# A list of 16 blocks for the recurrent part of a hybrid decoder block: projections two blocks ahead, dealt out between the levels, four value tiles a block, 64 keys at level 32

## The chip, the core and the metric

One core of a Trainium2 chip runs the whole program in one launch. The metric is the time on the device in microseconds (us), lower is better. Names used below: PE is TensorE (matmuls; PEld its weight loads), DVE is VectorE, ACT is ScalarE, POOL is GpSimd, SP is SyncE, which here only starts DMA transfers. Each engine works through its own queue in the order of the program and waits on semaphores for the others.

## The reference

The block takes x (2048 x 1024), norms it, projects it to 4096 columns, and runs two mixers beside each other: a gated linear recurrence (4 heads of 128) and a mixture of dilated window attentions (8 heads of 64). Both are gated, joined, projected and normed. All in float32. The part that the change touches is the recurrence:

```python
def hgrn2_mixer(q, f_logit, i, lb):
    log_f = jnp.logaddexp(jnp.log(lb), jnp.log1p(-lb) + jax.nn.log_sigmoid(f_logit))
    k = -jnp.expm1(log_f)
    q = jax.nn.silu(q)
    ...
    def step(state, inp):
        qc, kc, vc, gc = inp
        b = jnp.cumsum(gc, axis=2)
        o_inter = jnp.einsum('bhck,bhkv->bhcv', qc * jnp.exp(b), state)
        diff = b[:, :, :, None, :] - b[:, :, None, :, :]
        decay = jnp.exp(jnp.where(causal, diff, -jnp.inf))
        scores = jnp.einsum('bhtk,bhtsk,bhsk->bhts', qc, decay, kc)
        o_intra = jnp.einsum('bhts,bhsv->bhtv', scores, vc)
        ...
        new_state = jnp.exp(b_last[:, :, 0, :])[..., None] * state + \
            jnp.einsum('bhsk,bhsv->bhkv', k_dec, vc)
        return new_state, o_inter + o_intra
```

Behind it the readout is normed per head, multiplied by a gain and by silu of a gate z.

## The kernel before

The program has a prologue (the norm of x, its transposes, and the values and gates of head 0), the recurrent part, a short dense part (values of the attention), the attention and the output projection. Every float32 projection is done as three matmuls per 128 rows of depth on operands split in a high and a low half: hi by hi, hi by lo, lo by hi (lines 632 to 634), 24 matmuls in a group.

The recurrent part has four units, one per head. A unit has four blocks of 512 time steps, each of four chunks of 128. The order of the work is a list, `HG_STEPS`, that every engine walks; each engine does its share of a step:

- P: the queries of a block into bank 0 and its forget gates into bank 1, 24 matmuls of 512 columns each (PE). ACT takes the sigmoid of the queries (line 1024), DVE multiplies them (`q_read`).
- K: ACT takes two sigmoids of the forget gates (1032, 1033), POOL scales them (1249, 1250).
- L: DVE builds the decays and the scaled queries and keys for the five levels (half widths 4, 8, 16, 32, 64), lines 1440 to 1503, and signals `lev_ready` at its end.
- M: PE turns the keys (693) into bank 4, multiplies keys by queries for the five levels (704; 701 three times; 707), alternating between banks 2 and 3, and multiplies keys by values (716). DVE takes each level out of its bank (1516, 1521, 1524/1525, 1527) and says so with `lev_read`, which PE waits for two levels later; then it carries the states on (1535). ACT copies the turned keys out (1037).
- O: PE reads out (724, 726) to bank 6; ACT squares (1043); POOL takes the root (1258, 1260). Z: DVE norms and gates (1545) and SP stores.
- T: one value tile of the next unit: 24 matmuls of 256 columns (PE), into bank 7 for even tiles and bank 4 for odd ones; ACT copies it out and takes the sigmoid (987, 988, `sig_done`); in units 0 to 2 POOL gates it (1199, 1201, `gated`), in unit 3 (the tiles are the attention's first values) it does not; SP stores it. A tile may start when the tile two before it is out.

M needs bank 4 for the turned keys, so it waits for the last odd tile in front of it: `pe.wait_ge(sig_done, u * 16 + (16 + odd_before("M", b)))`. The numbers of tiles in front of the four M steps of a unit are 5, 7, 9 and 15, so the last tile before an M is always an even one, in bank 7.

The weights come in pieces: SP loads one of two staging buffers (362, `load_piece`), ACT makes the high half (972, `split_hi`), POOL the low half (1186, `split_lo`). The pieces of the values (slot 0) go in at P of block 0. Those of the next unit's queries and forget gates (slot 1) go in at the value tiles 8, 10, 11 and 13, behind the last P of the unit: SP starts a piece's load ahead of that tile's store, ACT splits it behind that tile's copy. A unit ends with DVE's, ACT's and POOL's steps for block 3; the next one begins with P for block 0 and P for block 1 one behind the other.

Of the kernel before, what the change touches and what calls it, by code (L numbers as in the profile page):

```python
# [11 lines left out]
ALU = mybir.AluOpType  # L12
ACT = mybir.ActivationFunctionType

P = 128
# [8 lines left out]
GC = 256  # L24
# [18 lines left out]
HG_STEPS = ([("P", 0), ("K", 0), ("L", 0), ("P", 1)] + [("T", t) for t in range(5)]  # L43
            + [("M", 0), ("K", 1), ("L", 1), ("P", 2), ("O", 0), ("T", 5), ("T", 6)]
            + [("M", 1), ("Z", 0), ("K", 2), ("L", 2), ("P", 3), ("O", 1), ("T", 7), ("T", 8)]
            + [("M", 2), ("Z", 1), ("K", 3), ("L", 3), ("T", 9), ("O", 2)] + [("T", t) for t in range(10, 15)]
            + [("M", 3), ("Z", 2), ("T", 15), ("O", 3), ("Z", 3)])
SPLIT_AT = {"prologue": (1, 4, 7, 10), "hgrn": (8, 10, 11, 13)}


def tiles_before(kind, b):

    return sum(k == "T" for k, _ in HG_STEPS[:HG_STEPS.index((kind, b))])


def odd_before(kind, b):

    return tiles_before(kind, b) // 2 * 2


def blocks_before(kind, tile):

    return sum(k == kind for k, _ in HG_STEPS[:HG_STEPS.index(("T", tile))])

# [41 lines left out]
def build(nc, x, w_groups, w_units, w_out, norm_w, gate_g, lb_logits, final_w, rope, near_mask, far_mask, tri_masks, out):  # L106
# [7 lines left out]
    with ExitStack() as ctx:  # L114
# [155 lines left out]
        passed_sp, passed_dve, passed_pool = sem("passed_sp"), sem("passed_dve"), sem("passed_pool")  # L270
        rs_half, dve_step, pool_step = sem("rs_half"), sem("dve_step"), sem("pool_step")
# [78 lines left out]
        def _(sp):  # L350
# [45 lines left out]
            for step in range(TILES + 5):  # L396
                if step >= 5:
                    phase1_store(0, step - 5)
                if step - 3 in SPLIT_AT["prologue"]:
                    load_piece(1, SPLIT_AT["prologue"].index(step - 3))  # L400
# [4 lines left out]
            def hg_unit(u, last):  # L405
                def load_vg(b):
                    if b == 0:
                        after(vg_stored[0], u * 128 + 128)
                        after(vg_stored[1], u * 128 + 128)
                    after(out_stored[b % 2], u * 32 + (16 * (b // 2) + ONE))  # L410
                    src = vg_dram[bass.ds(u, 1), b * BT:(b + 1) * BT, :]
                    sp.dma_start(vg_blk[b % 2], src.rearrange("a (c t) n -> (a t) c n", c=CH))\
                        .then_inc(vg_loaded[b % 2], 16)

                for kind, i in HG_STEPS:
                    if kind == "P":
                        if i == 0:
                            load_piece(2 * u + 2, 0)
                            load_piece(2 * u + 2, 1)
                            load_vg(0)  # L420
                            load_piece(2 * u + 2, 2)
                            load_piece(2 * u + 2, 3)
                            load_vg(1)
                    elif kind == "Z":
                        after((out_done0, out_done1)[i % 2], u * 2 + (i // 2 + 1 + ONE))
                        dst = mixed_dram[i * BT:(i + 1) * BT, bass.ds(u * P, P)]
                        sp.dma_start(dst.rearrange("(c t) n -> t c n", c=CH), vg_blk[i % 2][:, :, P:GC])\
                            .then_inc(out_stored[i % 2], 16)
                        if i < 2:
                            load_vg(i + 2)  # L430
                    elif kind == "T":
# [1367 lines left out]
```

## Time and profile before

| what | us |
|---|---|
| median of 3 runs | 1357.95 (1350.57 to 1358.93) |
| the profiled execution's own time | 1354.28 |
| its span, first to last instruction | 1352.3 |
| recurrent part on PE, first P to the end of the last O | 496.2 (81.97 to 578.18) |
| granted clock of PE, mean | 0.996 of 2.4 GHz |

The profile is one execution. The busy time of PE counts a matmul from its start to its modelled end, and the ends overlap with the next starts; so the distance between starts is what a matmul costs, and the text works with these. "idle before" stands in brackets behind a row with the one that ended it. Between the span and the execution's own time lie 2.0 us that the change doesn't touch.

### The profile page before, as it was taken

The page shows a single profiled execution, that of the slowest core. Times are in us where ns is not written, and L with a number is a line of the kernel's source. Part 1 is how long each engine was busy: PE and PEld are TensorE (multiplying, and loading weights), DVE is VectorE, ACT ScalarE, POOL GpSimd, SP SyncE. Part 2 cuts the span into 40 slices and gives each one's busy share as a digit, 9 for nine tenths or more (in the row PEclk, how much of TensorE's full clock was granted, in tenths as well). Part 3 has the DMA queues.
Part 4 walks back from the last instruction along what each step waited for, and adds up shares of the span by engine and source line. Part 5 has one row for each costly group of instructions (what it writes and reads, how often), then busy time and mean ns, then how long its engine had stood idle before and what let it go on. Part 6 is the DMA issues. An engine that isn't in the chain of part 4 may idle for free.

```text
span 1352.3 us, 23456 instructions
## 1 busy us (share of the span) xinstructions
PE 1300.5 (96%) x8520; PEld 1138.6 (84%) x8520; DVE 711.5 (53%) x1885; ACT 464.2 (34%) x1328; POOL 436.3 (32%) x441
## 2 busy tenths in 40 slices
PE   5999999999999999999999999999999999999997
PEld 5989998988889799999878877887788877878886
DVE  5837783776578378720445545544455456333332
ACT  5721122212212211221445445544545457411111
POOL 5742343333424312230134433443343344102000
PEclk9999999999999999999999999999999999999999
DMA  6520123013202301234355545554545566535431
GB/s 207 164 82 20 40 79 86 24 48 93 71 17 78 106 20 32 87 113 112 75 141 134 126 104 142 134 126 108 141 131 124 140 175 182 176 119 182 135 117 63
DMA packets 121714, 143.89 MB, mean 106 GB/s; under 512 B 20352, under 2 KB 86400, under 8 KB 121600
## 3 DMA queue, kind: packets, MB, share of 16 engines
q1 hardware_dynamic: 119200, 138.46, 36.5%
q10 hardware_dynamic: 2400, 3.93, 1.1%
q8 instruction: 69, 1.13, 0.4%
q14 instruction: 45, 0.37, 0.1%
HBM read 87.56 MB, written 29.62 MB: 87 GB/s over the span
## 4 chain that ended last, share of the span: by engine, by line
PE 76%; DMA 9%; DVE 8%; issue 2%; POOL 2%; ACT 2%; SPq 1%; ACTq 0%; DVEq 0%; POOLq 0%
PE bank L632 9%; PE bank L634 8%; PE bank L633 8%; PE bank L764 5%; PE bank L766 5%; PE bank L765 5%; PE bank L792 4%; PE bank L794 4%; PE bank L793 4%; DMA qd<-turned 4%; PE bank L871 3%; DMA stage<-in_w_groups 3%; PE bank L924 3%; PE bank L862 2%; PE bank L701 2%
## 5 line engine op out<-in xcount | busy, mean ns | idle before, releaser
L632 PE MATMUL bank<-w_hi,u_hi 128*128 128x256 f32 x768 | 221.2, 288 | 2.0 <-POOL w_lo L1186 1.5
L633 PE MATMUL bank<-w_lo,u_hi 128*128 128x256 f32 x768 | 218.1, 284 | 0.0
L634 PE MATMUL bank<-w_hi,u_lo 128*128 128x256 f32 x768 | 218.1, 284 | 0.0
L1368 DVE TENSOR_TENSOR room<-room 128x256 f32<-128x256 f32 (+6 forms) x386 | 135.2, 397 | 40.3 <-POOL room L1250 36.8
L632 PEld LDWEIGHTS bank<-w_hi,u_hi 128*128 128x128 f32 x768 | 148.1, 193 | 4.2 <-DVE u_lo L1368 1.7
L633 PEld LDWEIGHTS bank<-w_lo,u_hi 128*128 128x128 f32 x768 | 148.2, 193 | 0.2
L634 PEld LDWEIGHTS bank<-w_hi,u_lo 128*128 128x128 f32 x768 | 148.0, 193 | 0.0
L764 PE MATMUL bank<-u_hi,w_hi 128*128 128x512 f32 x256 | 108.7, 425 | 0.0
L1368 DVE TENSOR_TENSOR t<-bank,tab 128x512 f32<-128x512 f32 x64 | 42.6, 687 | 123.8 <-DMA tab<-in_rope 52.6
L632 PE MATMUL bank<-u_hi,w_hi 128*128 128x512 f32 x256 | 101.5, 397 | 5.2 <-ACT room L1033 2.4
L1282 POOL TENSOR_TENSOR r<-t,t 64x512 f32<-64x512 f32 x16 | 35.0, 2189 | 219.5 <-DVE w L1636 208.5
L766 PE MATMUL bank<-u_hi,w_lo 128*128 128x512 f32 x256 | 102.1, 399 | 0.0
L792 PE MATMUL bank<-u_hi,mT_hi 128*128 128x512 f32 x256 | 101.9, 398 | 0.0
L765 PE MATMUL bank<-u_lo,w_hi 128*128 128x512 f32 x256 | 101.7, 397 | 0.0
L794 PE MATMUL bank<-u_hi,mT_lo 128*128 128x512 f32 x256 | 100.0, 391 | 0.0
L634 PE MATMUL bank<-u_hi,w_lo 128*128 128x512 f32 x256 | 99.9, 390 | 0.0
L793 PE MATMUL bank<-u_lo,mT_hi 128*128 128x512 f32 x256 | 99.7, 390 | 0.0
L633 PE MATMUL bank<-u_lo,w_hi 128*128 128x512 f32 x256 | 99.6, 389 | 0.0
L1088 ACT COPY pT<-bank 128x512 f32<-128x512 f32 x60 | 35.3, 588 | 176.7 <-PE bank L885 176.7
L1605 DVE CUSTOM_DVE_ANT_0 p_near<-bank,near_m 128x256 f32<-128x256 f32 (+1 forms) x128 | 48.1, 411 | 85.3 <-PE bank L885 57.2
L871 PE MATMUL bank<-ks,qd 128*128 128x128 f32 (+3 forms) x256 | 88.6, 350 | 0.0
L1186 POOL TENSOR_TENSOR w_lo<-stage,w_hi 128x512 fp32r<-128x512 f32 x44 | 58.3, 1331 | 84.6 <-ACT w_hi L972 84.6
(169 smaller groups left out, 2936.0 us busy)
## 6 DMA issues: line engine op xcount, KB each, us to landing
qd<-turned SPq DMA_DIRECT2D x64, 256.0 KB, 4.7
stage<-in_w_groups SPq DMA_DIRECT2D x44, 256.0 KB, 3.9
room<-in_x SPq DMA_DIRECT2D x16, 512.0 KB, 4.4
values_gates<-vg_tile SPq DMA_DIRECT2D x64, 128.0 KB, 1.7
room<-values_gates SPq DMA_DIRECT2D x16, 512.0 KB, 4.7
tab<-in_rope SPq DMA_DIRECT2D x16, 512.0 KB, 5.7
wide<-mix_weights SPq DMA_DIRECT2D x32, 256.0 KB, 3.9
xr<-in_x SPq DMA_DIRECT2D x16, 512.0 KB, 4.9
```

What stands on the lines that cost most here:

```text
L632: nc.tensor.matmul(dst, lhs_hi(k), rhs_hi(k), start=(k == 0), stop=False)
L633: nc.tensor.matmul(dst, lhs_hi(k), rhs_lo(k), start=False, stop=False)
L634: last = nc.tensor.matmul(dst, lhs_lo(k), rhs_hi(k), start=False, stop=(k == KT_N - 1))
L764: yield nc.tensor.matmul(bk[:, :], wh[:, k, :], u_hi[:, k, sl], start=(k == 0), stop=False)
L765: yield nc.tensor.matmul(bk[:, :], wh[:, k, :], u_lo[:, k, sl], start=False, stop=False)
L766: last = nc.tensor.matmul(bk[:, :], wl[:, k, :], u_hi[:, k, sl], start=False, stop=(k == KT_N - 1))
L792: yield nc.tensor.matmul(bk[:, :], mT_hi[t % 2][:, k, :], wo_hi[half][:, k, :], start=(k == 0), stop=False)
L793: yield nc.tensor.matmul(bk[:, :], mT_hi[t % 2][:, k, :], wo_lo[half][:, k, :], start=False, stop=False)
L794: last = nc.tensor.matmul(bk[:, :], mT_lo[t % 2][:, k, :], wo_hi[half][:, k, :], start=False, stop=(k == KT_N - 1))
L871: last = nc.tensor.matmul(bank[2 + h][:, 0:P * (g + 1)], q[h][:, z, j::CH], keys, start=(z == 0), stop=(z == 1))
L1186: nc.gpsimd.tensor_tensor(w_lo[slot][:, 2 * i:2 * i + 2, :], stage[i % 2][:, :, :], w_hi[slot][:, 2 * i:2 * i + 2, :].bitcast(F32), ALU.su ...
L1368: return nc.vector.tensor_tensor(dst, a_, b_, op)
```

## The change

The list becomes one of 16 blocks over all units, without a loop over units. For block n (unit u, block b) it has: M; K and L of n+1; P of n+2; O; the value tiles; Z. At the seams of the units the next unit's P's now stand in the last two blocks of this one. The value tiles of a unit are dealt 4, 4, 4, 4 to its blocks (unit 0: 4 in front, then 3 a block; unit 3: 2, 2, 6, 6). The numbers of tiles in front of the M steps are now 4, 7, 10, 13, then 16, 20, 24 and so on by 4 up to 48, then 50, 52, 58. The two splits have steps of their own: G and V (load and split of the value weights), H and W (load and split of the query and forget weights).

```diff
+def hg_steps():
+    steps = [("N", 0, 0), ("G", 0, 0), ("G", 0, 1), ("P", 0, 0)] + [("V", 0, i) for i in range(2)]
+    steps += [("G", 0, 2), ("G", 0, 3), ("K", 0, 0), ("L", 0, 0), ("P", 0, 1)]
+    steps += [("V", 0, 2), ("V", 0, 3)] + [("T", 0, t) for t in range(4)]
...
+        if b == 1:
+            steps += [("H", u, 0), ("H", u, 1)]
+        steps.append(("O", u, b))
+        if b == 1:
+            steps += [("W", u, 0), ("W", u, 1), tiles[0], ("H", u, 2), ("W", u, 2), tiles[1], ("H", u, 3), ("W", u, 3)]
+            tiles = tiles[2:]
...
-                        pe.wait_ge(sig_done, u * 16 + (16 + odd_before("M", b)))
+                pe.wait_ge(sig_done, TILES + steps_before("T", ("M", u, b)) // 2 * 2)
...
+                        if l == COMPACT:
+                            last = nc.tensor.matmul(bank[2 + l % 2][0:64, c * 64:(c + 1) * 64], ka[:, c * P:c * P + 64],
+                                                    qa[:, c * P + 64:(c + 1) * P], start=True, stop=True)
...
+                    last.then_inc(lev_mm, 1)
+                    run(itertools.islice(beside, many))
```

Level 32 multiplies 64 keys instead of 128 (COMPACT is 3), for which DVE packs the keys and queries of that level otherwise; its copies keep their sizes. `beside` are the matmuls of the next step on PE: behind each of the five levels stand 3 of the 24 query matmuls of block n+2, or 5 of a value tile's 24 in blocks 14 and 15; the rest follow behind the matmuls of the values.

PE at block 1 of unit 0, in front of and in its M. Before (room is the recurrent part's memory; the level matmuls follow each other):

```order
L693 MATMUL bank4<-ident_57,room_63 128x128 [waits sig_done,kt_read,lev_ready]
L693 MATMUL bank4<-ident_57,room_63 128x128 x3
L704 MATMUL bank2<-room_63 128x128 [waits lev_read]
L704 MATMUL bank2<-room_63 128x128 x3
L701 MATMUL bank3<-room_63 128x64 [waits lev_read]
L701 MATMUL bank3<-room_63 128x64 x3
L701 MATMUL bank2<-room_63 128x64 [waits lev_read]
L701 MATMUL bank2<-room_63 128x64 x3
L701 MATMUL bank3<-room_63 128x64 [waits lev_read]
```

And now, from the same first row:

```order
L718 MATMUL bank4<-ident_57,room_63 128x128 [waits sig_done,kt_read,lev_ready]
L718 MATMUL bank4<-ident_57,room_63 128x128 x3
L732 MATMUL bank2<-room_63 128x128 [waits lev_read]
L732 MATMUL bank2<-room_63 128x128 x3
L648 MATMUL bank0<-u_hi_49,w_hi1_52 128x512 [waits q_read]
L649 MATMUL bank0<-u_lo_50,w_hi1_52 128x512
L650 MATMUL bank0<-u_hi_49,w_lo1_54 128x512
L729 MATMUL bank3<-room_63 128x64 [waits lev_read]
L729 MATMUL bank3<-room_63 128x64 x3
L648 MATMUL bank0<-u_hi_49,w_hi1_52 128x512
```

Three query matmuls (648 to 650 are the old 632 to 634) have moved in between two levels.

ACT at the splits of the query and forget weights (CAST into w_hi1) and the value tiles (COPY and ACTIVATE). Before, from the second piece on:

```order
L972 CAST w_hi1_52<-stage1_56 128x512 [waits w_landed1,f_ready]
L987 COPY vg_tile1_59<-bank4 128x256 [waits vg_stored1,vz_ready]
L988 ACTIVATE sg_tile1_61<-bank4 128x128
L972 CAST w_hi1_52<-stage0_55 128x512 [waits w_landed0,f_ready]
L987 COPY vg_tile0_58<-bank7 128x256 [waits vg_stored0,vz_ready]
L988 ACTIVATE sg_tile0_60<-bank7 128x128
L987 COPY vg_tile1_59<-bank4 128x256 [waits vg_stored1,vz_ready]
L988 ACTIVATE sg_tile1_61<-bank4 128x128
L972 CAST w_hi1_52<-stage1_56 128x512 [waits w_landed1,f_ready]
L987 COPY vg_tile0_58<-bank7 128x256 [waits vg_stored0,vz_ready]
```

Now, in unit 1, all four pieces and the four tiles of block 1, and the copy of the keys of block 2:

```order
L1015 CAST w_hi1_52<-stage0_55 128x512 [waits w_landed0,f_ready]
L1015 CAST w_hi1_52<-stage1_56 128x512 [waits w_landed1]
L1030 COPY vg_tile0_58<-bank7 128x256 [waits vg_stored0,vz_ready]
L1031 ACTIVATE sg_tile0_60<-bank7 128x128
L1015 CAST w_hi1_52<-stage0_55 128x512 [waits w_landed0]
L1030 COPY vg_tile1_59<-bank4 128x256 [waits vg_stored1,vz_ready]
L1031 ACTIVATE sg_tile1_61<-bank4 128x128
L1015 CAST w_hi1_52<-stage1_56 128x512 [waits w_landed1]
L1030 COPY vg_tile0_58<-bank7 128x256 [waits vg_stored0,vz_ready]
L1031 ACTIVATE sg_tile0_60<-bank7 128x128
L1030 COPY vg_tile1_59<-bank4 128x256 [waits vg_stored1,vz_ready]
L1077 COPY room_63<-bank4 128x512 [waits u_mm,kt_mm]
```

The third and the fourth piece now stand in front of the second and of the third tile, inside one block.

SP at the same place in unit 1. Before, from the first of those pieces on:

```order
L362 DMA stage0_55<-in_w_groups 128x512 [waits lo_done]
L372 DMA values_gates<-vg_tile0_58 128x256 [waits gated]
L427 DMA mixed<-room_63 128x4x128 [waits out_done1]
L412 DMA room_63<-values_gates 128x4x256 [waits out_stored1]
L372 DMA values_gates<-vg_tile1_59 128x256 [waits gated]
L362 DMA stage1_56<-in_w_groups 128x512 [waits lo_done]
L372 DMA values_gates<-vg_tile0_58 128x256 [waits gated]
L362 DMA stage0_55<-in_w_groups 128x512 [waits lo_done]
```

Now:

```order
L387 DMA stage0_55<-in_w_groups 128x512 [waits lo_done]
L387 DMA stage1_56<-in_w_groups 128x512 [waits lo_done]
L397 DMA values_gates<-vg_tile0_58 128x256 [waits gated]
L387 DMA stage0_55<-in_w_groups 128x512 [waits lo_done]
L397 DMA values_gates<-vg_tile1_59 128x256 [waits gated]
L387 DMA stage1_56<-in_w_groups 128x512 [waits lo_done]
L397 DMA values_gates<-vg_tile0_58 128x256 [waits gated]
```

Two pieces are loaded ahead of the block's first tile store; the third stands behind the first store and the fourth behind the second.

## Rows read from the trace of the kernel before

**Rows 1.** Unit 2: busy of PE, PEld, DVE, ACT, POOL and (instructions), PEclk, DMA share, GB/s

```profile
330.00:455.00 125.00, 121.37 (x850) 111.52 (x849) 82.41 (x212) 26.14 (x88) 44.80 (x60) 1.00 0.20 60
```

**Rows 2.** What PE waited for in the recurrent part: us in total, times, longest

```profile
PE bank L693 <- DVEq L1503: 4.5, 3, 1.6
PE bank L632 <- ACT room L1033: 2.4, 3, 1.2
PE bank L632 <- DVE room L1368: 2.2, 3, 1.0
PE bank L716 <- ACT room L1037: 0.7, 1, 0.7
```

**Rows 3.** Timeline of PE, M of block 2 in unit 0: start, us, what, xcount

```profile
167.11 0.60 PE L693 MATMUL bank<-ident,room 128*128 128x128 f32 x4
167.55 1.06 PE L704 MATMUL bank<-room 128*128 128x128 f32 x8
168.44 3.08 PE L701 MATMUL bank<-room 128*128 128x64 f32 x24
171.45 0.68 PE L707 MATMUL bank<-room 128*64 128x64 f32 x8
172.06 1.16 PE L716 MATMUL bank<-room 128*128 128x128 f32 x8
```

**Rows 4.** Timeline of PE: first matmul of P, first of T, first of M

```profile
81.97 0.47 PE L632 MATMUL bank<-u_hi,w_hi 128*128 128x512 f32 x1 [0.69 <-issue]
...
103.84 0.28 PE L632 MATMUL bank<-w_hi,u_hi 128*128 128x256 f32 x1
...
118.24 0.60 PE L693 MATMUL bank<-ident,room 128*128 128x128 f32 x4
```

**Rows 5.** Timelines of PE and ACT at the end of a value tile

```profile
202.63 0.28 PE L634 MATMUL bank<-w_hi,u_lo 128*128 128x256 f32 x1
202.95 0.37 ACT L987 COPY vg_tile<-bank 128x256 f32<-128x256 f32 x1 [7.32 <-PE bank L634]
203.22 0.28 ACT L988 ACTIVATE sg_tile<-bank 128x128 f32<-128x128 f32 x1
```

**Rows 6.** Timelines of ACT and POOL, unit 1: readout, gate, the two halves of a piece

```profile
303.48 0.28 ACT L1043 ACTIVATE room<-bank 128x128 f32<-128x128 f32 x1 [1.54 <-PE bank L726]
305.13 1.04 POOL L1260 TENSOR_TENSOR room<-room 128x4 f32<-128x4 f32 x1
302.02 0.46 POOL L1199 TENSOR_TENSOR vg_tile<-vg_tile,sg_tile 128x128 f32<-128x128 f32 x1 [1.23 <-ACT sg_tile L988]
312.22 0.62 ACT L972 CAST w_hi<-stage 128x512 fp32r<-128x512 f32 x1 [1.06 <-DMA stage<-in_w_groups]
320.34 1.28 POOL L1186 TENSOR_TENSOR w_lo<-stage,w_hi 128x512 fp32r<-128x512 f32 x1 [3.45 <-ACT w_hi L972]
```

**Rows 7.** The page, DMA issues: count, KB each, median us from issue to landing

```profile
stage<-in_w_groups SPq DMA_DIRECT2D x44, 256.0 KB, 3.9
```

**Rows 8.** Timeline of DVE, unit 1: M of block 0, L of block 1

```profile
244.39 0.73 DVE L1516 COPY_PREDICATED room<-room,bank 128x512 f32<-128x512 int32 x1 [3.17 <-PE bank L704]
...
250.72 0.43 DVE L1368 TENSOR_TENSOR room<-room 128x256 f32<-128x256 f32 x1 [0.31 <-DVE room L1535]
...
263.91 0.28 DVE L1501 COPY room<-room 128x256 f32<-128x256 f32 x1
```

**Rows 9.** Timeline of DVE, unit 1: L of block 3, first, a copy within, last

```profile
301.19 0.42 DVE L1368 TENSOR_TENSOR room<-room 128x256 f32<-128x256 f32 x1
...
310.94 1.39 DVE L1489 COPY room<-room 128x256 f32<-128x256 f32 x1
...
319.06 0.28 DVE L1501 COPY room<-room 128x256 f32<-128x256 f32 x1
```

**Rows 10.** Two stretches of the attention, columns as in rows 1

```profile
700.90:703.40 2.50, 0.04 (x1) 0.00 (x0) 0.00 (x0) 1.06 (x3) 1.88 (x2) 1.00 0.93 198
703.40:706.80 3.40, 3.36 (x10) 3.07 (x11) 1.29 (x2) 0.00 (x0) 0.61 (x1) 0.50 0.12 36
```

More of the change, by code:

```diff
@@ L40 @@
 ONE = 1
[L43 to L48, printed above, removed]
@@ L732, in _, with queries @@
-            for u in range(HG_UNITS):
-                hg_unit(u)
+            COMPACT = 3
+            def queries(u, b):
+                if b == 0:
+                    pe.wait_ge(lo_done, u * 8 + 8)
+                    if u == 0:
+                        pe.wait_ge(sig_done, TILES)
+                sl = slice(b * BT, (b + 1) * BT)
+                pe.wait_ge(q_read, u * 4 + (b + ONE))
+                yield from split_matmuls(bank[0][:, :], lambda k: w_hi[1][:, k, 0:P], lambda k: w_lo[1][:, k, 0:P],
+                                         lambda k: u_hi[:, k, sl], lambda k: u_lo[:, k, sl], q_ready)
@@ new lines, in read_out @@
+            def read_out(u, b):
+                pe.wait_ge(st_ready, u * 4 + (b + 1 + ONE))
+                pe.wait_ge(out_done0, u * 2 + (b + 1) // 2 + ONE)
+                pe.wait_ge(out_done1, u * 2 + (b // 2 + ONE))
+                for c in range(CH):
+                    nc.tensor.matmul(bank[6][:, c * P:(c + 1) * P], st[:, c, :], vg_blk[b % 2][:, c, 0:P],
+                                     start=True, stop=False)
+                    last = nc.tensor.matmul(bank[6][:, c * P:(c + 1) * P], q_in[:, c * P:(c + 1) * P],
+                                            states[b % 2][:, c, :], start=False, stop=True)
+                last.then_inc(o_mm, 1)
@@ new lines, in value_tile @@
+            def value_tile(u, t):
+                yield from phase1_tile(u + 1, t, "hgrn")
+            started = set()
+            for at_, (kind, u, b) in enumerate(HG_STEPS):
+                if kind == "P":
+                    if (kind, u, b) not in started:
+                        run(queries(u, b))
+                    run(forgets(u, b))
+                elif kind == "M":
+                    after_it = next((k, v, z) for k, v, z in HG_STEPS[at_ + 1:] if k in "PT")
+                    started.add(after_it)
+                    if after_it[0] == "P":
+                        scan_block(u, b, queries(*after_it[1:]), 3)
+                    else:
+                        scan_block(u, b, value_tile(*after_it[1:]), 5)
+                elif kind == "O":
+                    read_out(u, b)
+                elif kind == "T" and (kind, u, b) not in started:
+                    run(value_tile(u, b))
```

379 lines of the change are left out of this document (187 added, 192 removed).

## The prediction

> **What bounds the kernel now.** I read the busy times by stretch first, then the list of waits, then the timelines. In unit 2 PE is busy 121.4 of 125.0 us, DVE 82.4, POOL 44.8, at full clock [rows 1]: PE sets the pace. Its waits in the recurrent part are few: 4.5 us for the end of L (L1503) in front of block 3 of three units, 2.4 + 2.2 us at three seams between units, where two P's in a row share bank 0 and bank 1, and 0.7 us once, 9.8 in all [rows 2]. Starts show the rest. A P matmul takes (103.84 - 81.97) / 96 = 0.228 us, a T matmul (118.24 - 103.84) / 120 = 0.120 us [rows 4]. In M, level 4 takes 0.89 us for 8 records (a plain float32 matmul leaves two), 0.111 each; the next three levels take 3.01 us for 24, where 24 x 0.111 would be 2.67; level 64, with 64 keys, takes 0.61 for 8, 0.076 each [rows 3].
>
> **What goes.** (a) The waits: the seams (4.6) vanish, since P of n+2 no longer follows P of n+1 directly; the waits for L (4.5) vanish if L is done within a block (below); the 0.7 too. After each such wait the first matmul restarts later than the wait says; I put 0.3 us for each of nine, an estimate from the 0.34 us below. Together 9.8 + 2.7 = 12.5 us. (b) The levels: PE enters level 16 only when DVE has taken level 4 out of bank 2; that is the 3.01 - 2.67 = 0.34 us. With 0.7 us of query matmuls behind each level it is hidden: 16 x 0.34 = 5.4 us. (c) Level 32 with 64 keys: at best it loses what level 64 shows against level 16, 8 x (0.111 - 0.076) = 0.28 us. Level 64's 0.61 holds a restart of its own of about 0.1 us, so I take 0.4: 16 x 0.4 = 6.4 us; bounds 0 (the strided queries were not the cost) and 7. (d) Dealing out: more changes between kinds of matmul, ten a block. From level 4 to level 8 the change costs nothing visible [rows 3], and a restart costs 0.1 to 0.2. Bounds 0 and 16 x 0.5 = 8 us; I take 2.5, nearer to the row that shows nothing. Gain: 12.5 + 5.4 + 6.4 - 2.5 = 21.8 us.
>
> **What the block's length does to DVE.** DVE takes 250.72 - 244.39 = 6.3 us for M and 264.19 - 250.72 = 13.5 us for L when POOL is quiet [rows 8]. With five groups of query matmuls in between, M ends some 3 us later on PE (5 x 3 x 0.228, less the wait of (b)), so from the start of M to `lev_ready` I count 1.3 + 6.3 + 3 + 13.5 = 24 us. On PE a block has M 5.0, P 48 x 0.228 = 10.9, O 16 x 0.111 = 1.8 and four tiles 4 x 24 x 0.120 = 11.5: 29.2 us, so L is in time by 5 us; with three tiles (unit 0) by 2; with two (unit 3) PE has 23.5 and the two are level. L took 319.34 - 301.19 = 18.2 us where POOL split pieces and gated tiles beside it; a copy that takes 0.28 took 1.39 [rows 8, 9]. That case would end the slack (third rival). The Trainium skill says why (SBUF — State Buffer, "SBUF: two separate sides"): DVE and GpSimd share one port pair under an exclusive lock, so one waits for the whole of the other's instruction. The trace agrees as far as a copy of 0.28 us took 1.39 beside a split of POOL. It changes no term here, since in the middle units 5 us of slack cover 4.7.
>
> **What comes new, first: the last tile in front of M.** M waits for `sig_done` of the last odd tile. Before, the last tile in front of M was always even and cost nothing. Now the counts are 4, 7, 10, 13, 16, 20 and so on: even in 14 of 16 blocks. The last matmul of a tile starts at 202.63, and ACT's sigmoid ends at 203.50 [rows 5]; without the wait the next matmul would start 0.12 later. So 0.87 - 0.12 plus the restart of 0.1: 0.85 us. Ten of these blocks don't fall under the next term, and PE waits for the last tile once more at the end (the wait is there before too, but O stood in front of it): 11 x 0.85 = 9.4 us.
>
> **What comes new, second: pieces 3 and 4 of the query weights.** This is the largest term. They are split on ACT between the tiles of block 1, in front of the second and third tile, and SP starts their loads only behind the stores of the first and second tile. Let t = 0 be the end of P(u,3) on PE, in unit 1 or 2:
> - PE: O until 1.8, first tile until 4.7, second until 7.6, third until 10.4.
> - ACT starts its squares 0.3 behind O, and POOL's root ends 306.17 - 303.48 = 2.7 later [rows 6]: 4.8. Then POOL makes two low halves, 2 x 1.28: 7.3, and gates the first tile, 2 x 0.46: 8.2. Only then SP stores it and starts piece 3, about 8.7.
> - It lands 3.9 later [rows 7], 12.6. ACT has waited for it in front of the second tile; high half 0.62, copy and sigmoid 0.55: the second tile is out at 13.7. The fourth tile needs that. PE wanted to start it at 10.4 and starts at 13.8.
> - POOL: low half until 14.6, two gates until 15.5; SP starts piece 4 at 16.0; it lands at 19.9. ACT: high half 20.4, third tile 21.0, fourth tile 21.6. M needs the fourth.
> PE would have entered M at 1.8 + 4 x 2.88 = 13.3 and enters at 21.6: 8.3 us, in units 1 and 2. In unit 0, with three tiles in the block, it would have entered at 10.4 and does at 21.0: 10.6. In unit 3 there are two tiles and no gating (SP stores behind ACT): piece 3 starts at 6.1, the second tile is out at 11.1, and PE is ready at 7.6: 3.5. Piece 4 is then waited for beside M and costs nothing, as PE needs ACT's copy of the keys 7 us into M. Sum: 10.6 + 8.3 + 8.3 + 3.5 = 30.7 us. Bounds: 0 if the loads were early enough, and 36 if every DVE operation beside POOL's halves stretches them as in rows 9. Queued behind the waiting ACT are the tile copies, behind the waiting SP the next tile stores; nobody else.
>
> **Third: the clock.** In the attention PE stood for 2.5 us and came back at a granted clock of 0.50, 1.2 GHz, for 3.4 us [rows 10]; the stalls here are 3.4 to 10.6 us. 3.4 us at half the speed lose 1.7. Four stalls in front of an M, 1.5 each as PE does not use all of it: 6 us; bounds 0 (the shorter waits of rows 2 left the clock at 1.00, rows 1) and 10. The Trainium skill (TensorE: Matmul & The Clock Gate, "Why this matters for your kernels") advises against idle gaps between bursts of matmuls because the clock returns to half; rows 10 agree, and by it the splits' order costs twice, as I have it.
>
> **The sum** against the profiled execution's own time: 1354.3 - 21.8 + 9.4 + 30.7 + 6 = 1378.6. That execution lies 3.7 below the median shown (1357.95) and within the runs' spread; I forecast 1379 us, 1.6 to 1.8% slower. PE's loss of 46 us in waits is twice what the change wins. Everything behind the recurrent part (dense part, attention) shifts with it: the pieces for the dense tiles are started behind the last tile as before, with the 21.9 us of two projections as their cover.
>
> **The rivals.**
> 1. Faster: the third and fourth piece are covered. If SP starts them early enough that ACT doesn't stand in front of the second and third tile, 30.7 and 6 go and 1354.3 - 21.8 + 9.4 = 1341.9 is left. Deciding point: piece 4 landed before t = 11. Speaks for it: before, the same four pieces cost PE nothing that rows 2 name. Against it: then each had one or more tiles more between them and was started ahead of its tile's store. Chance 0.15.
> 2. About the same: the stall is there but half of it, since POOL takes its halves and gates in another rhythm or the root comes earlier, and the clock stays up: 1354.3 - 21.8 + 9.4 + 15 = 1356.9. Chance 0.2.
> 3. Slower still: L stretches to 18.2 us where POOL works beside it, so that the cycle is 28.7 us; in unit 0 (26.3 us of PE) two blocks lose 2.4 and in unit 3 (23.5) two blocks lose 5, less the 0.85 of each: +12, 1391. Speaks for it rows 9, against it that POOL is quiet in unit 3, where nothing is gated. Chance 0.15.
> 4. Dealing out costs its upper bound, or 64 keys bring nothing: +6, 1385. This lies in the forecast's own range, 1366 to 1393.
>
> **How the numbers follow.** The forecast has 0.5. The range for 8 in 10 reaches down through rival 2 and up past rival 3: 1350 to 1395. A measurement of this kernel tells about 1% (13.6 us) from no change. Slower by over 1%, above 1371.5: nearly all of the forecast, and rival 3, 0.63. Faster by over 1%, below 1344.4: most of rival 1, 0.12. Between: 0.25.
>
> **What would show it.** Right: in the list of waits, PE's first matmul of M (L718) waits for ACT's sigmoid of the tiles (L1031), some 0.7 us ten times and 5 to 11 us in front of block 2 of units 0 to 2; before the fourth tile (L648) a wait of 3 us; ACT's cast (L1015) waits for the staging DMA 6 us twice a unit; a granted clock of 0.5 for 3.4 us behind these. The waits for L1503 and those at the seams are gone, and level 32 takes 0.06 to 0.08 us a record. Wrong: no wait above 2 us on L718, and a recurrent part shorter than 490 us; or L718 waiting for L's end in most blocks.

## The result, and the profile after

The changed kernel took 1384.36 us in the median of 6 runs (1375.44 to 1386.16); the kernel before took 1352.81 beside it (1350.43 to 1358.93). The ratio is 1.0205, with a 95% interval of 1.0181 to 1.0229: slower by about 2%. The profiled execution took 1375.44 us, its span 1373.6, the mean granted clock 0.989 (before 0.996). It is the fastest of the six, 8.9 us below the median; the five others had a lower mean clock, 0.984 to 0.987. All that follows on stretches and waits is told of this one execution, so it accounts for the 21.2 us between the two profiled executions (1354.28 and 1375.44), not for the 31.6 between the medians.

First, where the time went. Two windows of the changed kernel: the recurrent part on PE up to the first matmul of the dense part, and the rest (columns as in [rows 1]):

```profile
81.58:603.78 522.20, 489.25 (x3393) 443.85 (x3393) 320.34 (x848) 102.15 (x336) 158.33 (x206) 0.97 0.18 57
603.78:1373.60 769.82, 746.43 (x4616) 626.11 (x4616) 329.03 (x964) 312.95 (x901) 226.45 (x157) 1.00 0.48 131
```

The same two windows of the kernel before:

```profile
81.97:578.18 496.21, 484.66 (x3392) 446.22 (x3393) 324.01 (x844) 101.16 (x328) 159.58 (x204) 1.00 0.20 60
578.18:1352.30 774.12, 748.89 (x4619) 628.11 (x4617) 331.01 (x968) 314.13 (x909) 228.05 (x159) 0.99 0.48 131
```

The recurrent part is 26.0 us longer, with hardly more busy time: PE stood. The rest is 4.3 us shorter. Two stretches of 3.4 us each at a clock of 0.50 in the attention [rows 10 show one] did not come in this execution, which can explain up to 3.4 us of it.

What PE waited for in the recurrent part of the changed kernel (us in total, times, longest), where [rows 2] stood before:

```profile
PE bank L718 <- ACT sg_tile L1031: 22.1, 11, 10.2
PE bank L648 <- ACT sg_tile L1031: 6.5, 2, 3.3
PE bank L718 <- DVEq L1543: 2.7, 1, 2.7
```

All waits of [rows 2] for the end of L, for the seams and for the copied keys are gone. M (L718) now waits for the sigmoid of a value tile: three times long (10.2, 4.1 and 2.0 in front of block 2 of units 0, 2 and 1), eight times 0.73. In unit 3, where a tile has no sigmoid, it waits twice 0.55 for the copy. Block 2 of unit 3 waits for L's end (2.7).

The stall of block 1 in unit 1. SP, the two tile stores and the loads of pieces 3 and 4:

```profile
294.28 0.33 SPq L397 DMA_DIRECT2D values_gates<-vg_tile  x1
294.65 0.43 SPq L387 DMA_DIRECT2D stage<-in_w_groups  x1
301.18 0.33 SPq L397 DMA_DIRECT2D values_gates<-vg_tile  x1
301.55 0.43 SPq L387 DMA_DIRECT2D stage<-in_w_groups  x1
```

ACT in the same stretch:

```profile
298.27 0.62 ACT L1015 CAST w_hi<-stage 128x512 fp32r<-128x512 f32 x1 [7.30 <-DMA stage<-in_w_groups]
298.79 0.36 ACT L1030 COPY vg_tile<-bank 128x256 f32<-128x256 f32 x1
...
305.21 0.62 ACT L1015 CAST w_hi<-stage 128x512 fp32r<-128x512 f32 x1 [5.88 <-DMA stage<-in_w_groups]
```

And PE, the fourth tile and M:

```profile
299.39 0.58 PE L648 MATMUL bank<-w_hi,u_hi 128*128 128x256 f32 x1 [3.25 <-ACT sg_tile L1031]
...
306.87 0.52 PE L718 MATMUL bank<-ident,room 128*128 128x128 f32 x3 [1.99 <-ACT sg_tile L1031]
```

Read them across the engines: the first store leaves at 294.28, the load behind it at 294.65, ACT sits 7.30 us at the head of its queue until it lands, and the second tile, long in its bank, is copied only then (298.79). PE's fourth tile starts at once behind the sigmoid of the second. The same again for piece 4. The prediction had t = 0 at the end of P, here 285.57: start of piece 3's load 8.7 (measured 9.1), second tile out 13.7 (13.8), M 21.6 (21.3).

The clock in the changed kernel: the three stretches at the low level, and one middle block for comparison (columns as above; the last but two is the granted clock):

```profile
172.40:186.10 13.70, 5.78 (x24) 5.52 (x25) 0.74 (x1) 3.55 (x9) 6.50 (x8) 0.50 0.21 59
298.70:305.50 6.80, 5.49 (x24) 5.20 (x24) 0.00 (x0) 0.92 (x4) 2.10 (x3) 0.50 0.24 58
435.20:442.10 6.90, 4.99 (x21) 4.73 (x22) 0.74 (x1) 3.08 (x8) 5.00 (x7) 0.51 0.25 78
343.00:374.00 31.00, 30.27 (x215) 27.39 (x215) 19.30 (x54) 6.44 (x22) 11.08 (x15) 1.00 0.19 62
```

PE was granted 1.2 GHz instead of 2.4 for 27 us in all, each time while it stood or just after.

Last, M with the query matmuls dealt out, unit 0, block 1, where [rows 3] had levels alone:

```profile
143.36 1.06 PE L732 MATMUL bank<-room 128*128 128x128 f32 x8
144.17 0.48 PE L648 MATMUL bank<-u_hi,w_hi 128*128 128x512 f32 x1
...
144.96 1.00 PE L729 MATMUL bank<-room 128*128 128x64 f32 x8
...
148.22 0.68 PE L725 MATMUL bank<-room 128*64 128x64 f32 x8
148.82 0.51 PE L648 MATMUL bank<-u_hi,w_hi 128*128 128x512 f32 x1
...
149.73 0.68 PE L735 MATMUL bank<-room 128*64 128x64 f32 x8
```

Starts: a level of eight records takes 144.17 - 143.36 = 0.81, level 32 (L725) 148.82 - 148.22 = 0.60, but a group of three query matmuls takes 144.96 - 144.17 = 0.79 and, between levels 32 and 64, 149.73 - 148.82 = 0.91, where 3 x 0.228 = 0.68. M and P together take 16.62 us in this block (142.93 to 159.55); before they took 16.87 in the same place. So all the work on the levels brought 0.25 us in this block.

### The profile page after: what moved, and what is told of

The parts are those of the page before. It is cut to its first block, busy times and chain, and to the rows that moved or that the text cites. A ratio compares the mean times of both kernels' runs of the same rounds, so it can differ in the third digit from the quotient of the medians.

```text
span 1373.6 us, 23453 instructions
## 1 busy us (share of the span) xinstructions
PE 1301.9 (95%) x8520; PEld 1133.3 (83%) x8520; DVE 706.2 (51%) x1885; ACT 464.1 (34%) x1328; POOL 434.0 (32%) x441
## 4 chain that ended last, share of the span: by engine, by line
PE 81%; DMA 7%; DVE 4%; POOL 2%; ACT 2%; issue 2%; SPq 2%; ACTq 0%; POOLq 0%; DVEq 0%
PE bank L648 11%; PE bank L650 10%; PE bank L649 10%; PE bank L811 5%; PE bank L813 5%; PE bank L812 5%; PE bank L839 4%; PE bank L841 4%; PE bank L840 4%; PE bank L914 3%; DMA qd<-turned 3%; PE bank L967 3%; DMA stage<-in_w_groups 3%; PE bank L905 2%; PE bank L729 2%
## 5 line engine op out<-in xcount | busy, mean ns | idle before, releaser
L648 PE MATMUL bank<-w_hi,u_hi 128*128 128x256 f32 x768 | 222.4, 290 | 10.2 <-ACT sg_tile L1031 6.5
L1402 DVE TENSOR_TENSOR room<-room 128x256 f32<-128x256 f32 (+6 forms) x386 | 132.3, 390 | 14.7 <-POOL room L1287 7.8
L648 PE MATMUL bank<-u_hi,w_hi 128*128 128x512 f32 x256 | 108.7, 425 | 0.7 <-issue 0.7
L811 PE MATMUL bank<-u_hi,w_hi 128*128 128x512 f32 x256 | 108.1, 422 | 0.5 <-issue 0.5
L914 PEld LDWEIGHTS bank<-ks,qd 128*128 128x128 f32 x256 | 78.8, 310 | 5.0 <-issue 3.2
```

Of the source, the lines that this page charges most:

```text
L648: yield nc.tensor.matmul(dst, lhs_hi(k), rhs_hi(k), start=(k == 0), stop=False)
L811: yield nc.tensor.matmul(bk[:, :], wh[:, k, :], u_hi[:, k, sl], start=(k == 0), stop=False)
L914: last = nc.tensor.matmul(bank[2 + h][:, 0:P * (g + 1)], q[h][:, z, j::CH], keys, start=(z == 0), stop=(z == 1))
L1402: return nc.vector.tensor_tensor(dst, a_, b_, op)
```

## The experiments

Two theories stood at the start. The prediction's: the loss is SP's late start of pieces 3 and 4 (30.7), the wait for the last tile (9.4) and the clock (6), against a gain of 21.8. Its rivals: ACT or POOL is simply full there, whoever loads when; the waits in front of M are a cost of the bank itself; L is the next to be late; the dealing costs what it hides. Since the rest of the program differs by a few us from one execution to the next (stretches at low clock in the attention come and go), I compare the recurrent part on PE beside the medians.

**1. The loads earlier (e1_early).**

```diff
-            steps += [("W", u, 0), ("W", u, 1), tiles[0], ("H", u, 2), ("W", u, 2), tiles[1], ("H", u, 3), ("W", u, 3)]
-            tiles = tiles[2:]
+            steps += [("W", u, 0), ("W", u, 1), ("H", u, 2), ("H", u, 3)] + tiles[:2] + [("W", u, 2)] + tiles[2:3] + [("W", u, 3)]
+            tiles = tiles[3:]
```

> The changed kernel with one edit: in block 1 of each unit the loads and the splits of pieces 3 and 4 of the query and forget weights stand elsewhere in the list. SP starts both loads in front of the block's first tile store; ACT splits piece 3 in front of the third tile and piece 4 in front of the fourth (or behind). Nothing else moves. Theory (the stall is SP's late start of the loads behind the tile stores): the waits of L718 for sg_tile L1031 of 10.2, 8 and 8 us in front of block 2 go, the cast L1015 waits under 1 us for its DMA, the stretches at a granted clock of 0.50 go too; the recurrent part on PE falls from 522.2 to about 492 us and the time from 1384 (1375 in the profiled run) to about 1347 to 1352, no slower than the kernel before (1352.8). Rival A (the stall is ACT's load of work, or POOL's halves and gates, whatever SP does): PE still loses 3 to 8 us a unit there, time 1362 to 1375. Rival B (the clock alone costs more than the waits): the clock goes and more than 34 us with it, below 1345.

Measured: 1355.68 us (10 runs), ratio to before 1.0004 (0.998 to 1.0028). The recurrent part fell from 522.2 to 498.1. PE's waits (the last line, for w_lo, belongs to the dense part behind it):

```profile
PE bank L718 <- ACT sg_tile L1031: 7.4, 10, 0.8
PE bank L718 <- DVEq L1543: 4.5, 2, 2.7
PE bank L648 <- POOL w_lo L1223: 2.9, 1, 2.9
```

No wait for a tile is above 0.8 us: the long ones are gone, and the recurrent part is 24.1 us shorter. Rival A and rival B fall. The edit moves four entries of each unit's list, though: the two loads (H), and the two splits (W) on ACT and POOL to behind the second and the third tile. It does not separate the two. A row of ACT, unit 1, where P ends at 276.03, speaks for the loads:

```profile
285.27 0.62 ACT L1015 CAST w_hi<-stage 128x512 fp32r<-128x512 f32 x1 [0.96 <-DMA stage<-in_w_groups]
```

Piece 3 had landed 9.2 us behind the end of P, where the changed kernel has 12.7, and piece 4 was started at 283.79, 7.8 us behind it, against 16.0. Even with its cast in front of the second tile, that tile would have been out at 9.2 + 0.62 + 0.55 = 10.4, which is when PE wants the fourth tile. This is an estimate; no run moves the loads alone.

It stayed 4 us above what I expected, because other waits took over: in unit 0 M now waits for the end of L, and in units 0 and 3 a stretch at half clock follows the wait for L. DVE in unit 0:

```profile
153.87 0.43 DVE L1402 TENSOR_TENSOR room<-room 128x256 f32<-128x256 f32 x1 [0.31 <-DVE room L1575]
...
165.87 1.38 DVE L1527 COPY room<-room 128x256 f32<-128x256 f32 x1
...
171.37 0.28 DVE L1541 COPY room<-room 128x256 f32<-128x256 f32 x1
```

POOL beside it:

```profile
164.23 2.87 POOL L1223 TENSOR_TENSOR w_lo<-stage,w_hi 128x512 fp32r<-128x512 f32 x2
```

L takes 171.65 - 153.87 = 17.8 us, where it takes 13.5 with POOL quiet [rows 8]: the third rival's stretching, on a block with three tiles. L718 waits 1.8 us and M then runs partly at half clock. From its first matmul to the O behind it M and P take 18.42 us here instead of 16.65, and 13.00 instead of 11.37 in unit 3. In the changed kernel the late L of unit 0 cost nothing, as PE was standing for the tiles anyway.

**2. The tiles' banks changed (e2_banks).** M needs bank 4 only; which tile is in it is free to choose. The second pair of lines is the tile's own wait until ACT has copied the turned keys out of bank 4; it moves from the odd to the even tiles.

```diff
-"hgrn": (bank[7], bank[4])
+"hgrn": (bank[4], bank[7])
...
-                if beside == "hgrn" and t % 2:
+                if beside == "hgrn" and t % 2 == 0:
...
-                pe.wait_ge(sig_done, TILES + steps_before("T", ("M", u, b)) // 2 * 2)
+                pe.wait_ge(sig_done, TILES + (steps_before("T", ("M", u, b)) - 1) // 2 * 2 + 1)
```

> The changed kernel with one edit: the value tiles of the recurrent part change their banks, even tiles into bank 4 (which M needs for the turned keys), odd ones into bank 7. The loads of the weights stay late. 14 of 16 blocks have an even number of tiles in front of M, so the last one is odd and would now be free of the wait; the blocks with 7 and 13 gain it. Theory (each such wait costs 0.9 us, the T segments of 12.5 against 11.5 and of 9.6 against 8.7): time 7 to 8 us below the changed kernel, 1376 to 1378 against 1384, and no wait of 0.7 to 0.9 us on L718 but in blocks 1 and 3 of unit 0. In front of block 2 the long wait shrinks only by some 0.9, since the fourth tile itself starts late (or by up to 6 us more where the fourth tile's copy was what M waited for, if M no longer needs the fourth tile: it is split behind piece 4; then PE goes into M right behind the fourth tile, and the time falls to 1360 to 1368). Rival (the wait is a restart of the bank itself, which any matmul behind a tile pays): same time as the changed kernel, within 2 us.

Measured: 1385.71 us (4 runs), 1.0241 (1.02 to 1.0282): no gain. The recurrent part takes 525.7 us against 522.2. The short waits did go (a block of four tiles takes 11.60 us from the first tile to M, against 12.49), but PE ran into block 2 of unit 0 earlier, and stood inside M:

```profile
173.92 1.09 PE L718 MATMUL bank<-ident,room 128*128 128x128 f32 x4 [3.11 <-ACT sg_tile L1031]
...
181.32 0.79 PE L648 MATMUL bank<-u_hi,w_hi 128*128 128x512 f32 x1 [4.61 <-POOL w_lo L1223]
```

The query matmuls dealt into block 2 are those of the next unit's block 0, and they need piece 4's low half. The late piece has a second consumer, which the prediction had not named: in unit 0, taking away the tile wait only moves the stall by one place, from in front of M to behind level 4, where it also splits M. And the clock stayed low longer:

```profile
172.40:192.80 20.40, 14.28 (x57) 11.71 (x58) 2.84 (x8) 3.60 (x9) 6.47 (x8) 0.52 0.22 65
```

Together unit 0 lost 1.8 us there. In units 1 and 2 the fourth tile started late as before. The largest loss is in unit 3, 8.9 us: from M of block 2 to the O behind it PE takes 20.26 us, against 11.37. The tile dealt into that M is an even one, now in bank 4, so it waits for ACT's copy of the turned keys, and that copy stands behind the cast of the late piece 4:

```profile
553.32 0.62 ACT L1015 CAST w_hi<-stage 128x512 fp32r<-128x512 f32 x1 [4.26 <-DMA stage<-in_w_groups]
553.85 0.58 ACT L1077 COPY room<-bank 128x512 f32<-128x512 f32 x1
554.57 0.36 PE L648 MATMUL bank<-w_hi,u_hi 128*128 128x256 f32 x1 [2.82 <-ACT room L1077]
```

The granted clock was low for most of what followed (0.60 on average from 548.5 to 565.7). So the theory's size for the short waits held (0.89 each) and its forecast of the time did not: a shorter wait in front of a late piece was given back at the piece's next consumers.

**3. Both, and an even number of tiles in front of every M (e3_both).** Both diffs above, and

```diff
-HG_TILES = ((3, 3, 3, 3), (4, 4, 4, 4), (4, 4, 4, 4), (2, 2, 6, 6))
+HG_TILES = ((4, 2, 4, 2), (4, 4, 4, 4), (4, 4, 4, 4), (2, 2, 6, 6))
```

> The changed kernel with both edits, early loads of pieces 3 and 4 and the tiles' banks changed, and the tiles of unit 0 dealt 4, 2, 4, 2 instead of 3, 3, 3, 3, so that every block has an even number of tiles in front of its M. Theory (stall and waits for the last tile are all that the change lost): 30 + 9 + the clock's 3 go from 1384, so 1338 to 1344, about 1% below the kernel before (1352.8). In unit 0 the blocks with two tiles are short on PE (23.5 us), where the end of L may be waited for by 1 to 3 us. Rival (the freed time is given back, since DVE's L or POOL's gates are the next to be late): PE waits for DVEq of L's end in blocks 1 and 3 of unit 0 and elsewhere, 1350 to 1358.

Measured: 1357.18 us (9 runs), 1.0037 (1.0013 to 1.0062); the recurrent part 491.6. The rival was right. PE's waits:

```profile
PE bank L718 <- DVEq L1543: 8.0, 4, 4.6
PE bank L648 <- POOL w_lo L1223: 2.7, 1, 2.7
```

No wait for a tile is left, but I had put two tiles into the very block beside whose L the splits and gates run. The longest waits, in front of block 2 of units 0 and 3:

```profile
174.62 1.12 PE L718 MATMUL bank<-ident,room 128*128 128x128 f32 x4 [4.61 <-DVEq L1543]
...
522.28 1.11 PE L718 MATMUL bank<-ident,room 128*128 128x128 f32 x4 [2.65 <-DVEq L1543]
```

L718's four records last 1.1 us where they last 0.60 elsewhere: half clock behind each wait. Behind the first 48 matmuls of the dense part stand a wait for w_lo (2.7) and some 7 us at half clock too.

**4 and 5. The tiles where L is long; the dense weights earlier (e6_tiles, e7_dense).** The fourth kernel has only

```diff
-HG_TILES = ((4, 2, 4, 2), (4, 4, 4, 4), (4, 4, 4, 4), (2, 2, 6, 6))
+HG_TILES = ((2, 4, 4, 2), (4, 4, 4, 4), (4, 4, 4, 4), (2, 4, 6, 4))
```

> e3_both with one edit: the tiles of unit 0 dealt 2, 4, 4, 2 and those of unit 3 dealt 2, 4, 6, 4 (they were 4, 2, 4, 2 and 2, 2, 6, 6), so that block 1 of every unit, beside whose L the splits and gates run, has four tiles. Theory (in e3_both PE waits there for the end of L, 4.6 us in unit 0 and 2.7 in unit 3, and then works for some us at half clock, T segments of 10.60 and 8.65 against 5.8): both waits and both stretches of 0.50 go, the recurrent part falls from 491.6 to about 481 us and the time from 1357 to about 1346 to 1348; two-tile blocks elsewhere cost 0.5 each. Rival (the end of L is late in every two-tile block, wherever it stands, since the cycle of DVE is 24 us): the waits move to blocks 0 and 3, the time stays within 3 us of e3_both.

Measured: 1342.6 us (5 runs), 0.991 (0.9881 to 0.994); recurrent part 482.4. The two-tile blocks elsewhere wait 0.9 us or less, three times, so it is the work beside L in block 1 (POOL's splits, and in unit 0 its gates), and not DVE's cycle as such, that made the block behind it late. The fifth adds, in SP's step T:

```diff
+                    if u == HG_UNITS - 1 and i == TILES - 2:
+                        load_piece(2 * DENSE + 2, 0)
+                        load_piece(2 * DENSE + 2, 1)
                     phase1_store(u + 1, i, u == HG_UNITS - 1)
-                    if u == HG_UNITS - 1 and i == TILES - 1:
...
```

> e6_tiles with one edit: SP loads the first two pieces of the dense part's tile weights ahead of the store of the last but one value tile, not behind the last. Theory: the wait for w_lo at the start of the dense tiles (2.7 us in e3_both, with 5 us at half clock behind it) goes, 3 to 5 us less than e6_tiles, 1341 to 1344. Rival (the attention behind it waits for its own transfers and takes the gain back): within 1 us of e6_tiles.

Measured: 1337.17 us (6 runs), 0.9881 (0.9848 to 0.9914). The wait for w_lo is gone; the 48 matmuls in front of it, with the wait, take 11.00 us against 14.08. Of PE's waits for another engine in the recurrent part one line is left:

```profile
PE bank L718 <- DVEq L1543: 1.6, 3, 0.9
```

I ran this kernel again beside a later one:

> e7_dense unchanged, a second time, beside e11_one_group on one chip and to firm up its distance from the kernel before: 1.0 to 1.4% below it.

Measured: 1337.9 us (6 runs), 0.9904 (0.9885 to 0.9924).

**6. The 64 keys alone (e8_128keys).** The fifth kernel with level 32 on 128 keys again.

```diff
-                        if l == COMPACT:
-                            last = nc.tensor.matmul(bank[2 + l % 2][0:64, c * 64:(c + 1) * 64], ka[:, c * P:c * P + 64],
-                                                    qa[:, c * P + 64:(c + 1) * P], start=True, stop=True)
-                        elif 0 < l < LEVELS - 1:
+                        if 0 < l < LEVELS - 1:
```

> e7_dense with level 32 back to 128 keys (the packing undone, all else kept). Prediction's term (c): +6.4 us against e7_dense. Theory from the trace of the changed kernel (level 32 takes 0.61 us for 8 records, levels 8 and 16 take 0.81): 16 times 0.2, +3.2 us. Rival: 0, if the time of a level is set by something else.

Measured: 1340.72 us (6 runs), 0.9903 (0.9876 to 0.9929), against 0.9881: the intervals overlap. The recurrent part is 483.1 us against 481.8 and 482.0 in the two profiles of the fifth kernel, so the 64 keys bring some 1.1 to 1.3 us, by one profile against two. Why so little is in the timeline of M. Level 32 takes 0.81 there and not 0.61, as expected, but by the starts the groups of query matmuls in front of levels 32 and 64 take 0.78 and 0.87, where the kernel with 64 keys has 0.87 and 0.89. Level 16 and the matmuls of keys by values:

```profile
408.41 1.00 PE L726 MATMUL bank<-room 128*128 128x64 f32 x8
...
413.08 1.05 PE L742 MATMUL bank<-room 128*128 128x128 f32 x8
```

The kernel with 64 keys in the same place:

```profile
410.30 1.00 PE L729 MATMUL bank<-room 128*128 128x64 f32 x8
...
414.89 1.05 PE L745 MATMUL bank<-room 128*128 128x128 f32 x8
```

From level 16's first record to the matmuls of the values: 413.08 - 408.41 = 4.67 with 128 keys, 414.89 - 410.30 = 4.59 with 64. The 0.2 us in its own row is 0.08 in the block, 1.3 in 16: a group with 64 keys looks cheap in its row, and the group in front of it pays.

**7. Nothing dealt out (e9_undealt).** The fifth kernel with the counts 3 and 5 in the two calls of `scan_block` set to 0.

> e7_dense with nothing dealt between the levels: the 15 query matmuls (or tile matmuls in blocks 14 and 15) stand behind the matmuls of keys by values, as before. Prediction's terms (b) and (d): +5.4 for level 16's wait, -2.5 for the changes between kinds, so +2.9 us. Theory from the traces (M takes 13.4 us less in all than before, 3.2 of it the 64 keys, but the P matmuls that stand between levels take 10.5 more): dealing out is worth nothing, 0 within 1.5 us.

Measured: 1337.99 us (6 runs), 0.9876 (0.9848 to 0.9904): the same as the fifth kernel. Its M:

```profile
404.57 0.60 PE L718 MATMUL bank<-ident,room 128*128 128x128 f32 x4
...
405.90 2.20 PE L729 MATMUL bank<-room 128*128 128x64 f32 x16
408.03 0.68 PE L725 MATMUL bank<-room 128*64 128x64 f32 x8
...
410.37 0.48 PE L648 MATMUL bank<-u_hi,w_hi 128*128 128x512 f32 x1
```

M 5.80 and P 11.00 make 16.80 us, against 16.64 dealt out: the gain is 0.16 a block, or 2.6 us in 16, and the undealt kernel has M shorter, so L starts earlier and the waits of the two-tile blocks (1.6 and their restarts) vanish. The two cancel. The sums over the recurrent part, from start to start, say how: undealt, M's own matmuls take 92.8 us and the P's 175.8; dealt, 78.8 and 186.2, and the tiles 3.1 more (2.0 of it those waits, 1.0 the groups of blocks 14 and 15). Dealt, M is 14.0 shorter, of which only 5.4 are the wait in front of level 16 as the prediction reckons it, and the queries take 10.4 longer. In all the recurrent part takes 482.3 us undealt against 481.8.

**8. One group only (e11_one_group).** If only the wait in front of level 16 is worth hiding, one group does it.

```diff
-                    run(itertools.islice(beside, many))
+                    if l == 1:
+                        run(itertools.islice(beside, many))
```

> e7_dense with one group of three matmuls between levels, behind level 8, where all five levels had one. Theory (only the wait in front of level 16, 0.34 us, is worth hiding; each further group costs about 0.09 to 0.2 us in its first matmul and hides nothing): a block's M and P take about 16.5 us against 16.64 (five groups) and 16.80 (none), so 2 to 3 us less than e7_dense. Rival (each level then waits for DVE's reading of the level two before, 1.2 us a level): the wait moves to level 32 and 64 and the block takes 16.7 to 16.8, no gain.

Measured, on the fifth kernel: 1333.76 us (4 runs, 1332.75 to 1333.91), 0.9869 (0.985 to 0.9888), beside 1337.9 for the fifth itself. M:

```profile
402.62 0.63 PE L718 MATMUL bank<-ident,room 128*128 128x128 f32 x4
...
404.79 0.50 PE L648 MATMUL bank<-u_hi,w_hi 128*128 128x512 f32 x1
...
405.60 1.00 PE L729 MATMUL bank<-room 128*128 128x64 f32 x8
...
408.86 0.47 PE L648 MATMUL bank<-u_hi,w_hi 128*128 128x512 f32 x1
```

M and P take 16.50 us in most blocks (16.56 in this one), the recurrent part 478.1: 18.1 less than before. No wait for L or for a tile is left. It is the fastest version here: 1.3% below the kernel before, by its interval 1.1 to 1.5%. The ratio to before doesn't separate it from the fifth (the intervals overlap); beside it on the same chip its 4 runs (up to 1333.91) lie below all 6 of the fifth (from 1335.74).

**9. The price of the clock (e10_fill).** The changed kernel with idle matmuls, whose result nobody reads, in the long waits.

```diff
+                if b == 2:
+                    pe.wait_ge(lev_read, u * (4 * LEVELS) + b * LEVELS + 1)
+                    for _ in range((40, 20, 20, 0)[u]):
+                        nc.tensor.matmul(bank[2][:, :], w_hi[0][:, 0, 0:P], u_hi[:, 0, 0:BT], start=True, stop=True)
```

> The changed kernel with matmuls added whose result nobody reads: in front of M of block 2, 40 of them (128 x 512, 0.228 us each, 9.1 us) in unit 0 and 20 (4.6 us) in units 1 and 2, into bank 2. They lie within the waits for sg_tile (10.2, and some 5 us behind the fourth tile's 3.3), so PE works where it stood. Prediction's third term (the clock, 6 us in four stalls): the stretches at 0.50 go and with them up to 6 us, 1378 against 1384. Theory from the trace (a good part of the slow stretches lies within the waits themselves, so that only unit 0's M, 2.9 us, and a bit of unit 2's was lost): 2 to 4 us. Rival (the clock falls all the same, since the 3.3 us in front of the fourth tile stay): no gain, within 1 us.

Measured: 1379.59 us (4 runs), 1.022 (1.0192 to 1.0247), against 1.0205 for the changed kernel: the times can't tell. The profiles can, for one M. The window of unit 0's stall and M, with the fill and without it in the changed kernel:

```profile
170.40:189.42 19.02, 18.32 (x110) 15.07 (x108) 4.81 (x13) 3.72 (x9) 6.52 (x8) 1.00 0.30 82
```

```profile
170.40:189.42 19.02, 9.10 (x47) 8.18 (x48) 3.77 (x9) 3.71 (x9) 6.50 (x8) 0.64 0.27 78
```

With the fill PE keeps the full clock and M, up to the 16th query matmul, takes 189.41 - 180.36 = 9.05 us; without it 192.09 - 180.32 = 11.77. So the slow clock cost 2.7 us there, by the same reckoning 11.40 - 9.06 = 2.3 in unit 2, and nothing in unit 1, where the slow stretch lay in a tile that ACT was the later for. That is 5 us in three stalls. The kernel with the fill won back only 1.9 of it in the recurrent part (520.3 us). In unit 2 the clock fell just behind the unfilled 3.2 us in front of the fourth tile: the tile took 4.40 us instead of 2.97, the 20 idle matmuls behind it ended after M's own resources were there, and M started 9.05 us behind the tile's start instead of 7.21, which took 1.8 of the 2.4 that M then gained. In unit 3, without a fill, the clock fell this time too, and M cost 1.6 more. The rest of its program came out 5.1 us longer, so the 3.2 us between the spans (1376.8 and 1373.6) say nothing on the fill.

## Why the prediction was right

The forecast was 1379 us and the median is 1384.4; the recurrent part was to grow by 24.3 us and grew by 26.0. Term by term, on PE:

- **The waits that go (12.5).** Right. What PE took over the plain length before is 6.3 us at the three seams (23.87, 24.10 and 24.06 for 96 matmuls of 21.9), 5.2 in front of block 3 of three units (15.93, 16.26 and 16.23 against 14.4), 0.8 for the copied keys (9.82 against 9.05) and 0.9 for the four single tiles between M and O of block 2 (3.19 each, against 2.96 in block 3), 13.2 in all; the changed kernel has none of these.
- **Levels, 64 keys and dealing (5.4 + 6.4 - 2.5 = 9.3).** Wrong in size; the three together brought 0.25 us a block, 4 us. Two steps failed. "I take 0.4" for level 32 read the cost of a group off its own row; removed alone, the 64 keys are worth 1.1 to 1.3 us, not 6.4. And "from level 4 to level 8 the change costs nothing visible" was the wrong neighbour for the change from a level to a 512-column matmul: the groups cost 0.77 to 0.91 us for 0.68, 10.4 us in all, above my upper bound of 8. What the levels gain beyond (b) by not following each other directly (0.81 for eight records and not 0.89 or more; 14.0 us in all by experiment 7, the 64 keys left in on both sides, 5.4 of it the wait that I had) I had left out, and it nearly pays for that. With these sizes, and 1.0 for the groups of tile matmuls in blocks 14 and 15, the term is 14.0 + 1.2 - 10.4 - 1.0 = 3.8.
- **The last tile in front of M (11 x 0.85 = 9.4).** Right: eight of the waits are 0.73 each in the list and 0.9 by the starts (12.49 for four tiles against 11.60 in kernels without the wait), the three in and behind unit 3 0.7 by the starts, 9.2 us together.
- **Pieces 3 and 4 (10.6, 8.3, 8.3, 3.5).** Right: from the end of O to M, less the tiles' own length, 10.4, 8.0, 7.8 and 2.8 us, 29.0 for 30.7. In unit 3 there were two causes at once: the tile's copy and L both ended at 552.91, and M waited for both, so the loads alone would have gained nothing there. In experiment 1, with loads and splits moved, 22.4 of the 29.0 us went (2.0 in unit 0 and 2.8 in unit 3 are then L's end, the rest the last tile's wait), and the recurrent part fell by 24.1. The medians fell by more, 28.7 us, but the rest of the program differs between executions. That nobody else stands behind the late piece, as the prediction says, was wrong: the next unit's queries do, and so does ACT's copy of the turned keys, on which a tile in bank 4 waits (experiment 2). Both decide only once the first wait is cured.
- **The clock (6).** Right as to size, 5 measured. I had four stalls at 1.5; it was two at 2.5, one at nothing, and no low clock in unit 3.

The sum: -13.2 - 4 + 9.2 + 29.0 + 5 = 26.0, as measured. The 5 us that the levels didn't bring were made up by the rest of the program, 4.3 us shorter in this execution, so part of the closeness of the profiled time (1375.4 for 1378.6) is luck. Against the kernel before beside it the median grew by 31.6 us where 24.3 were forecast; what the other executions lost beyond the profiled one was not traced. Their mean clock was lower, which points to more stretches at half clock.

Of the rivals, the first (covered loads) and the second (half a stall) are excluded by the rows of unit 1. The third, L stretched by POOL, is real, also in unit 3, where the prediction took POOL to be quiet: POOL makes its low halves there too, L took 15.7 us, and it showed as 2.7 us, and in the first and the third experiment it became the bound as soon as the stall was gone. The fourth was half right: the 64 keys bring nearly nothing, and the dealing costs over its bound, but what the levels save covers it.

The prediction took from the Trainium skill (TensorE: Matmul & The Clock Gate, "Why this matters for your kernels") that idle gaps bring the clock down. The ninth experiment bears it out: with PE busy in the gap of unit 0 the granted clock stays 1.00, with the gap it is 0.64 over the same 19 us. The rows also show that the price is small where the slow stretch lies mostly within the wait itself: 5 us lost for 27 at half clock.

## What to carry to other kernels

When steps are merged into one list, check for every transfer what stands in front of its start on the issuing engine, and what stands behind its consumer: here two loads behind two stores, with their casts in front of two copies, cost 8 to 10 us in each of three units, and moving the loads and the splits gave 24 us back. Cure the late resource before the waits around it, and expect the next wait to appear: the end of L, hidden in the changed kernel, was the bound of the next two. Fill a gap only where the trace has one; here the four further groups between levels cost more than they hid (16.64 us a block against 16.50 with one group), and the cost of a short group must be read together with the groups on both sides of it.

## What the runs showed of the hardware that I had not expected

- Three 128 x 512 matmuls between groups of small ones take 0.79 us instead of 0.68, and 0.91 between the two levels with 64 keys; the levels beside them take 0.81 instead of 0.89. What one row wins the next one partly loses.
- A stall of 1.8 to 2.7 us in front of M was followed by a granted clock of 0.50 in the first and the third experiment (1.8 in unit 0 of the first, 2.7 in unit 3 of both), while in the changed kernel the one of 2.68 us in unit 3 did not: L718's four records last 0.63 there, against 1.1 in the third experiment.
- Executions of one kernel differ by 11 us and more, and the longer ones mostly show a lower granted clock: the kernel of experiment 5 took 1334.57 us at a mean of 0.998 and 1345.83 at 0.992, the kernel before 1349.11 at 0.998 and 1365.30 at 0.993. Below 1% I told my versions apart by the recurrent part, read from one profile each; the one kernel that was profiled twice had 481.8 and 482.0.
